# Block 2: context half of the norm on two engines, first transposition of a pair ahead of the scores, query evicted earlier, steps of the first and last column placed anew

## The chip, the cores and the metric

The kernel runs on one core of one Trainium2 chip. The time is device time of one execution, in microseconds (us); a lower one is better. Names of the engines: TensorE (PE, with PEld for its weight loads), VectorE (DVE), ScalarE (ACT), GpSimd (POOL), and SyncE (SP), which issues the weight transfers.

## What is computed

One sequence of 256 tokens of width 1024 goes through two blocks, all in float32. Block 1 (two layers of mixing and feed-forward) is not touched. Block 2 has four layers of kinds A, B, C, A, here called layers 0 to 3, on 256 latent tokens and 256 context tokens:

```
for i in range(4):                      # kinds A, B, C, A
    sh, sc, gt    = split(silu(c) @ ada_w[i] + ada_b[i], 3)
    shc, scc, gtc = split(silu(c_ctx) @ ada_w[i] + ada_b[i], 3)
    h  = rms_norm(x,  norm_g[i]) * (1 + sc)  + sh       # latent half
    hc = rms_norm(xc, norm_g[i]) * (1 + scc) + shc      # context half
    u, z   = split(h @ w_in)            # q, k, v and a gate z
    uc, zc = split(hc @ w_in)
    o, oc  = mixer(u, uc)               # q, k normed per head (A, C: rope), softmax(q k^T) v
    x  = x  + gt  * ((o  * silu(z))  @ w_out)
    xc = xc + gtc * ((oc * silu(zc)) @ w_out)           # not in the last layer
```

Kind A has 16 query heads on 4 key heads, kind B adds a neighbourhood bias, kind C subtracts a second softmax. The last layer needs no context output, so its queries are the 256 latent tokens alone.

## The kernel before

Everything is kept with features on the 128 partitions, in KC = 8 chunks of 128; T = 256 latent and C = 256 context tokens make N2 = 512 columns. Each matrix product is made of three passes (`product`, lines 456 to 460): high part of the weight by high and low part of the activation, and low part of the weight by the high part. So each weight tile has to be split: ACT rounds it to `w_hi` (L1018, `hi_parts`), POOL or DVE subtracts to `w_lo` (L298, `lo_parts`). Tiles come in one fixed order (`PLAN`) through a ring of four; three splits are kept. `chunk` yields after each of the eight k steps of a product, so that the steps can be dealt out between other PE work.

Each engine has its own program of which the order is written out by hand; semaphores connect them. An engine that waits holds all that stands behind it in its program.

**The norm** (`block2`, beginning). DVE multiplies x2 by the reciprocal norm, chunk by chunk (L1706, semaphore `normed`). ACT scales and shifts the latent half of each (L1233, `h_full`), POOL the context half (L2057, `h_ctx`). PE makes the v product from it (L740): its first quarter waits for `h_full` chunk by chunk, its third quarter for all of `h_ctx`. ACT then evicts a row of the next modulation (L1023) and rounds all to `h_hi` (L1240), DVE makes `h_lo` (L1709).

**The columns.** Attention goes over eight columns c (a pair of heads) and in each over NU units u: three token tiles by two heads, NU = 6, in layers 0 to 2; NU = 4 in layer 3. A pair is the two units 2p and 2p + 1. PE per unit (lines 857 to 908): at even u `scores` of both units of the pair (L781, L786), a part of the steps of the matrix products of the next query (`chunk`, "q chunk") and of the gate z (`gemm_part`), transposition of the probabilities of unit u - 2 (`to_keys`, L696) into the one bank `tb`, another part, and at odd u `values_both` of the pair before (L839, L845). `scores` waits until the exponentials of the two units before are done, `to_keys` until that unit's probabilities are normalised (`p_normed`) and the bank `tb` has been read (`t_read`). At u = NU - 2 PE makes the sums of squares of the next query (`q_sums`, L754), which wait for ACT's `q_sq`.

DVE per unit: the maxima of both scores (`biggest`, L1766 and L1763), at even u the copy of the pair's first transposition (`first_keys`, L1811), at odd u the two scalings (`normalise`, L1803); at u = NU - 2 and NU - 1 rope of the next query and its norm sum (`q_rms`, L1742), after which POOL raises it to the power (L2071). The first `biggest` of a column waits for that. ACT per unit: at even u the two exponentials (L1342, L1336), at odd u `second_keys` (L1305), the copy of the pair's second transposition, for which `values_both` waits; then, at u = NU // 2, `evac_q` of the next column: w_hi of a later tile, a square (L1245) and a scaled copy `raw` (L1248) of the query's bank. In kind C a pair gives one combined matrix (`combine`), `keys` (L1298) copies its transposition, and `subln` normalises the column before.

The last column also splits the gated outputs: ACT's `gated_high` (L1289), DVE's `split_gated` (L1844). FILL_SLOT is true in layers 0 to 2; there column 0 and 7 also carry a row of modulation, and `gemm_part` has steps of its own for them.

Of the kernel before, what the change touches and what calls it, by code (L numbers as in the profile page):

```python
# [19 lines left out]
KC = D // P  # L20
T = 256
C = 256
N2 = T + C
# [123 lines left out]
def build_program(nc, wall, consts, pos, x_in, ctx_in, nbias, y_out):  # L147
# [7 lines left out]
    with ExitStack() as stack:  # L155
# [277 lines left out]
        def _(pe):  # L433
# [271 lines left out]
            def block2(L):  # L705
# [151 lines left out]
                for c in range(KC):  # L857
# [22 lines left out]

                    def gemm_part():
                        nonlocal spot
                        if 0 < c < KC - 1 or not slot:
                            steps = (spot + 1) * count // parts - spot * count // parts
                        elif spot < parts // 2:
                            steps = KC // (parts // 2) + (spot < KC % (parts // 2))
                        else:
                            steps = (spot + 1) * 8 // parts - spot * 8 // parts
                        for _ in range(steps):
                            next(pieces, None)  # L890
                        spot += 1
                    for u in range(NU):
                        if u % 2 == 0:
                            scores(c, u)
                        gemm_part()
                        past = [(c, u)] + past[:3]
                        if past[2] and closes(kind, us[past[2][1]]):
                            to_keys(*past[2])
                        if kind != "C":
                            gemm_part()  # L900
                            if past[2] and u % 2:
                                values_both(past[2][0], past[2][1] // 2)
                        elif past[3] and closes(kind, us[past[3][1]]):
                            values(*past[3])
                        if kind == "C" and u == OT and c:
                            out_to_features(c - 1)
                        if u == NU - 2 and c + 1 < KC:
                            q_sums(c + 1)
# [59 lines left out]
        def _(act):  # L968
# [244 lines left out]
            def block2(L):  # L1213
# [17 lines left out]
                for m in range(KC):  # L1231
                    act.wait_ge(S["normed"], (5 + L) * KC + m + 1)
                    act.activation(h2[:, m, 0:T], h2[:, m, 0:T], ACT.Identity, bias=ada[:, L, m, 0:1], scale=mod[:, m, 0:1])\  # L1233
                        .then_inc(S["h_full"], 1)
                for _ in range(FILL_RMS[L]):
                    ada_row_out()
                act.wait_ge(S["h_full"], (6 + L) * KC)
                for m in range(KC):
                    act.wait_ge(S["h_ctx"], L * KC + m + 1)
                    act.activation(h_hi[:, m, :], h2[:, m, :], ACT.Copy).then_inc(S["h_hi_ready"], 1)  # L1240

                def evac_qk(R, dst_sq, gain, signal, N, at=None):
# [114 lines left out]
                for c in range(KC):  # L1357
                    for u in range(NU):
                        if u == 0 and c >= (2 if slot else 1):
                            evac_z(c - slot)  # L1360
                        if u % 2 == 0:
                            exponential(c, u)
                            exponential(c, u + 1)
# [4 lines left out]
                        else:  # L1368
# [3 lines left out]
                                output_squares(past[3][0])  # L1372
                            if u == OT - 1 and c:
                                subln(c - 1)
                        if u == NU // 2 and c + 1 < KC:
                            evac_q(c + 1, early if c == 1 else None)
                            if c == 1 and slot:
                                ada_columns_out()
                        if u == NU // 2 and c == KC - 1 and slot:
                            evac_z(c)  # L1380
                        if c == KC - 1:
# [59 lines left out]
        def _(dve):  # L1441
# [244 lines left out]
            def block2(L):  # L1686
# [180 lines left out]
                past = [None] * 4  # L1867
                for c in range(KC):
                    for u in range(NU):
                        if u % 2 == 0:  # L1870
                            biggest(c, u)
                            biggest(c, u + 1)
                        if u == NU - 1 and c + 1 < KC:
                            q_end(c + 1)
                        past = [(c, u)] + past[:3]
                        if kind == "C" and u % 2:
                            combine(c, u)
                        if kind != "C":
                            if past[2] and u % 2 == 0:
                                first_keys(*past[2])  # L1880
                            if u % 2:
                                normalise(c, u - 1)
                                normalise(c, u)
                        elif past[3] and closes(kind, us[past[3][1]]):
                            output(*past[3])
# [3 lines left out]
                            q_start(c + 1)  # L1889
                        if u == NU - 1 and c + 1 < KC:  # L1890
                            q_rms(c + 1)
                        if c == KC - 1:
                            for i in splits_at(NU, u, FILL_SLOT[L], OT):
                                split_gated(i)
                last = [(KC - 1, u) for u in range(NU) if closes(kind, us[u])]
                if kind == "C":
                    output(*last[-2])
# [59 lines left out]
        def _(pool):  # L1957
# [81 lines left out]
            def block2(L):  # L2039
# [11 lines left out]
                if kind == "B":  # L2051
                    pool.wait_ge(S["h_full"], 6 * KC)
                    for head in range(4):
                        load_bias(head)
                for m in range(KC):
                    pool.wait_ge(S["normed"], (5 + L) * KC + m + 1)
                    pool.tensor_scalar(h2[:, m, T:N2], h2[:, m, T:N2], mod[:, m, 1:2], ada[:, L, m, 1:2], ALU.mult, ALU.add).then_inc(S["h_ctx"], 1)  # L2057
                def qz_tile(i):
# [276 lines left out]
```

## Time and profile before

| | |
|---|---|
| median of three runs | 2235.68 us (2224.66 to 2236.77) |
| the profiled execution | 2232.29 us, span 2230.5 us |
| PE, PEld | 91%, 77% of the span busy |
| DVE, ACT, POOL | 53%, 49%, 42% |
| granted PE clock, mean | 0.951 of full speed |
| block 2 | from about 938 us to the end |

The profile is of one execution. A line of the timeline has start, duration, engine, line of the program, operation, output and inputs with their forms, a count where several were merged, and in brackets the engine's idle time before it with what ended it. "ACTq L1251" is ACT's sequencer at a semaphore instruction on that line. The granted clock is a share of the full rate: 1.00 is 2.4 GHz, 0.50 is 1.2 GHz.

### The profile page before, as it was taken

Reading aid. Unit: us, or ns where it says so; the run is one execution under the profiler, and the core shown is the slowest. Engines: PE = TensorE matmul, PEld = TensorE weight load, DVE = VectorE, ACT = ScalarE, POOL = GpSimd, SP = SyncE. Lnnn points to the kernel's source line nnn. Section 1 sums busy time; section 2 is a strip of 40 time slices with the busy share of each in tenths; the row PEclk is TensorE's granted clock in tenths of the full one; section 3 lists DMA queues with packets and bytes.
Section 4 is the critical chain, followed back from the end, with each engine's and each line's share of the span. In section 5 each row is a group of like instructions: output and inputs, shape, how many; then the busy total and the mean of one; then the engine's idle time right before and its main releaser. Section 6 shows DMA issues by size and latency. Waiting matters only on the chain.

```text
span 2230.5 us, 39126 instructions
## 1 busy us (share of the span) xinstructions
PE 2036.7 (91%) x14528; PEld 1717.4 (77%) x14528; DVE 1187.7 (53%) x2582; ACT 1084.9 (49%) x2073; POOL 933.0 (42%) x598
## 2 busy tenths in 40 slices
PE   6899899988998999888999999998999899798787
PEld 5898799987987899776766886665788667567666
DVE  6854556658545566347673206667223766614553
ACT  5353566453634654454554336445334555535443
POOL 1574378004744682043452123443204455424443
PEclk9899999998999999999999999999999999899898
DMA  7353656653435566442123332222223211223211
GB/s 262 114 152 112 190 172 196 184 186 113 149 101 187 171 188 188 164 142 76 48 61 101 114 104 84 88 67 85 95 86 95 95 38 48 76 95 104 67 58 57
DMA packets 72991, 262.89 MB, mean 118 GB/s; under 512 B 8048, under 2 KB 10224, under 8 KB 72560
## 3 DMA queue, kind: packets, MB, share of 16 engines
q1 hardware_dynamic: 71536, 256.31, 36.6%
q0 software_dynamic: 1280, 4.20, 0.6%
q8 instruction: 116, 1.90, 0.4%
q14 instruction: 59, 0.48, 0.1%
HBM read 259.43 MB, written 1.05 MB: 117 GB/s over the span
## 4 chain that ended last, share of the span: by engine, by line
PE 68%; DVE 9%; issue 8%; POOL 7%; ACT 6%; DMA 1%; DVEq 0%; SPq 0%; ACTq 0%; POOLq 0%
PE gemm L458 15%; PE gemm L459 14%; PE gemm L460 14%; PE gemm L740 7%; POOL w_lo L298 3%; PE tbank L696 2%; PE score L781 2%; PE obank L839 2%; PE stat L703 1%; POOL rot L1970 1%; PE gemm L666 1%; PE stat L536 1%; ACT w_hi L1018 1%; PE stat L754 1%; PE score L786 1%
## 5 line engine op out<-in xcount | busy, mean ns | idle before, releaser
L298 POOL TENSOR_TENSOR w_lo<-ring,w_hi 128x1024 fp32r<-128x1024 f32 x262 | 628.6, 2401 | 721.8 <-ACT w_hi L1018 718.4
L458 PE MATMUL gemm<-g_hi,w_hi 128*128 128x256 f32 x1344 | 394.7, 294 | 29.2 <-DVE w_lo L298 10.8
L1018 ACT ACTIVATE w_hi<-ring 128x1024 fp32r<-128x1024 f32 x344 | 361.3, 1053 | 82.9 <-PE gemm L460 37.4
L458 PE MATMUL gemm<-h_hi,w_hi 128*128 128x512 f32 (+1 forms) x928 | 390.8, 421 | 4.7 <-POOL w_lo L298 4.7
L459 PE MATMUL gemm<-g_lo,w_hi 128*128 128x256 f32 x1344 | 384.0, 286 | 0.0
L460 PE MATMUL gemm<-g_hi,w_lo 128*128 128x256 f32 x1344 | 383.6, 285 | 0.0
L459 PE MATMUL gemm<-h_lo,w_hi 128*128 128x512 f32 (+1 forms) x928 | 352.6, 380 | 0.0
L460 PE MATMUL gemm<-h_hi,w_lo 128*128 128x512 f32 (+1 forms) x928 | 352.1, 379 | 0.0
L458 PEld LDWEIGHTS gemm<-g_hi,w_hi 128*128 128x128 f32 x1344 | 262.9, 196 | 47.7 <-issue 23.3
L460 PEld LDWEIGHTS gemm<-g_hi,w_lo 128*128 128x128 f32 x1344 | 264.2, 197 | 0.0
L459 PEld LDWEIGHTS gemm<-g_lo,w_hi 128*128 128x128 f32 x1344 | 263.3, 196 | 0.1
L458 PEld LDWEIGHTS gemm<-h_hi,w_hi 128*128 128x128 f32 x928 | 181.2, 195 | 92.1 <-issue 62.8
L460 PEld LDWEIGHTS gemm<-h_hi,w_lo 128*128 128x128 f32 x928 | 181.2, 195 | 34.3
L459 PEld LDWEIGHTS gemm<-h_lo,w_hi 128*128 128x128 f32 x928 | 182.0, 196 | 32.2 <-issue 8.4
L1342 ACT ACTIVATE pr<-score,small 128x512 f32<-128x512 f32 (+1 forms) x192 | 127.5, 669 | 160.3 <-DVE small L1768 158.4
L740 PE MATMUL gemm<-ring,arena 128*128 128x128 f32 x1280 | 158.1, 288 | 11.6 <-ACT arena L1233 9.9
L740 PEld LDWEIGHTS gemm<-ring,arena 128*128 128x128 f32 x1280 | 154.4, 201 | 15.2 <-DMA ring<-wall 12.5
L1766 DVE TENSOR_REDUCE small<-score 128x1 f32<-128x512 f32 (+1 forms) x144 | 98.6, 685 | 94.5 <-PE score L781 38.2
L298 DVE TENSOR_TENSOR w_lo<-ring,w_hi 128x1024 fp32r<-128x1024 f32 x82 | 104.0, 1274 | 52.7 <-ACT w_hi L1018 51.6
L696 PE MATMUL tbank<-cst,pr 128*128 128x128 f32 x560 | 89.7, 283 | 25.9 <-DVE pt L1811 25.8
L696 PEld LDWEIGHTS tbank<-cst,pr 128*128 128x128 f32 x560 | 67.7, 144 | 48.6 <-issue 39.1
L1905 DVE TENSOR_TENSOR x<-x,rot 128x512 f32<-128x512 f32 (+1 forms) x32 | 29.7, 927 | 140.4 <-ACTq L1419 140.4
(305 smaller groups left out, 3608.9 us busy)
## 6 DMA issues: line engine op xcount, KB each, us to landing
ring<-wall SPq DMA_DIRECT2D x478, 512.0 KB, 3.7
r<-nbias POOLq DMA_DIRECT2D x16, 256.0 KB, 2.9
cst<-consts SPq DMA_DIRECT2D x1, 2037.0 KB, 13.4
r<-x_t SPq DMA_DIRECT2D x1, 1024.0 KB, 5.8
x<-ctx_t SPq DMA_DIRECT2D x1, 1024.0 KB, 15.8
y_t<-x SPq DMA_DIRECT2D x4, 256.0 KB, 2.4
cst<-consts SPq DMA_DIRECT2D x1, 303.5 KB, 3.0
x<-pos SPq DMA_DIRECT2D x1, 128.0 KB, 2.0
```

The source lines that it names most:

```text
L298: eng.tensor_tensor(w_lo[:, q % SPLITS, :, :], ring[:, t % RING, :, :], w_hi[:, q % SPLITS, :, :].bitcast(F), ALU.subtract)\
L458: pe.matmul(out, w[0][:, k, :], x[0], start=start, stop=False)
L459: pe.matmul(out, w[0][:, k, :], x[1], start=False, stop=False)
L460: return pe.matmul(out, w[1][:, k, :], x[0], start=False, stop=stop)
L696: ins = pe.transpose(tb[:, j * P:(j + 1) * P], src(j), ident)
L740: ins = pe.matmul(out[:, t * P:(t + 1) * P], h2[:, k, t * P:(t + 1) * P], w[:, k, :], start=(k == 0), stop=(k == KC - 1))
L781: ins = pe.matmul(bk[:, :], q[:, t * P:(t + 1) * P], k, start=True, stop=True)
L839: ins = pe.matmul(rows(hh)[:, t * P:(t + 1) * P], v(hh, j), pt[:, hh, j * P:(j + 1) * P], start=(j == 0), stop=(j == 3))
L1018: act.activation(w_hi[:, q % SPLITS, :, :], ring[:, t % RING, :, :], ACT.Copy).then_inc(S["hi_ready"], 1)
L1342: ins = act.activation(dst[:, a:z], src[:, a:z], ACT.Exp, scale=rq, bias=NBm[:, 2 * i4 + q:2 * i4 + q + 1], accum_out=SUM[:, 2 * i4 + q:2 ...
L1766: seq(dve.tensor_reduce(MX[:, i2:i2 + w], bk[:, :] if t < 2 else bk[:, :].rearrange("p (a n) -> p a n", a=2), AX, ALU.max))
L1905: dve.tensor_tensor(x2[:, m, 0:NQ], x2[:, m, 0:NQ], rot[:, m % 2, 0:NQ], ALU.add).then_inc(S["x2_ready"], 1)
```

## The change

Four edits, all in block 2.

1. Norm: POOL does the context half of the even chunks alone; ACT does it for the odd chunks, each right behind the latent half of the same chunk. ACT waits once for all of `h_ctx` ahead of `h_hi`.
2. Kinds A and B: at even u PE transposes unit u - 2 ahead of the scores, where it stood behind them and a part of the products; DVE's `first_keys` stands ahead of `biggest` in the same way. Kind C keeps its order.
3. ACT's `evac_q` of the next column (with the ada columns in column 1) stands at the head of unit NU // 2: ahead of `second_keys` (`keys` and `subln` in kind C), and in layer 3 ahead of two exponentials.
4. First column of layers 0 to 2: the eight steps of the q chunk are made in the first third of the column, where they filled the first half. Last column: DVE makes the splits of the gated outputs of two units together at the odd one.

```diff
@@ PE, gemm_part
-                        if 0 < c < KC - 1 or not slot:
+                        if c == 0 and slot and spot < parts // 2:
+                            steps = KC * 3 // parts * (spot < parts // 3)
+                        elif 0 < c < KC - 1 or not slot:
@@ PE, units
                     for u in range(NU):
+                        past = [(c, u)] + past[:3]
                         if u % 2 == 0:
+                            if kind != "C" and past[2]:
+                                to_keys(*past[2])
                             scores(c, u)
                         gemm_part()
-                        past = [(c, u)] + past[:3]
-                        if past[2] and closes(kind, us[past[2][1]]):
+                        if past[2] and u % 2:
                             to_keys(*past[2])
@@ ACT, norm
+                    if m % 2:
+                        act.activation(h2[:, m, T:N2], h2[:, m, T:N2], ACT.Identity, bias=ada[:, L, m, 1:2], scale=mod[:, m, 1:2])\
+                            .then_inc(S["h_ctx"], 1)
                 for _ in range(FILL_RMS[L]):
                     ada_row_out()
                 act.wait_ge(S["h_full"], (6 + L) * KC)
+                act.wait_ge(S["h_ctx"], (L + 1) * KC)
                 for m in range(KC):
-                    act.wait_ge(S["h_ctx"], L * KC + m + 1)
@@ ACT, units
                         if u == 0 and c >= (2 if slot else 1):
                             evac_z(c - slot)
+                        if u == NU // 2 and c + 1 < KC:
+                            evac_q(c + 1, early if c == 1 else None)
+                            if c == 1 and slot:
+                                ada_columns_out()
                         if u % 2 == 0:
                             exponential(c, u)
                             exponential(c, u + 1)
...
-                        if u == NU // 2 and c + 1 < KC:
-                            evac_q(c + 1, early if c == 1 else None)
-                            if c == 1 and slot:
-                                ada_columns_out()
@@ DVE, units
+                        past = [(c, u)] + past[:3]
                         if u % 2 == 0:
+                            if kind != "C" and past[2]:
+                                first_keys(*past[2])
                             biggest(c, u)
                             biggest(c, u + 1)
...
-                        past = [(c, u)] + past[:3]
...
-                            if past[2] and u % 2 == 0:
-                                first_keys(*past[2])
...
-                        if c == KC - 1:
-                            for i in splits_at(NU, u, FILL_SLOT[L], OT):
-                                split_gated(i)
+                        if c == KC - 1 and u % 2:
+                            for v in (u - 1, u):
+                                for i in splits_at(NU, v, FILL_SLOT[L], OT):
+                                    split_gated(i)
@@ POOL, norm
-                for m in range(KC):
+                for m in range(0, KC, 2):
                     pool.wait_ge(S["normed"], (5 + L) * KC + m + 1)
```

## Rows read from the trace of the kernel before

**Rows 1.** Waits of PE: who waited for whom, us in total, times, longest.

```profile
PE stat L754 <- ACTq L1251: 26.8, 13, 2.9
PE tbank L696 <- DVE pt L1811: 25.8, 23, 4.1
```

**Rows 2.** Busy time by stretch: columns in layers 0, 1, 2, and six of 3.

```profile
core 0: us, PE busy (x) PEld busy (x) DVE busy (x) ACT busy (x) POOL busy (x), PEclk, DMA share, GB/s
1046.00:1067.70 21.70, 21.70 (x137) 15.44 (x137) 15.16 (x38) 11.55 (x26) 10.37 (x6) 1.00 0.17 49
1464.89:1488.04 23.15, 22.05 (x138) 15.38 (x137) 14.71 (x38) 11.38 (x26) 10.06 (x8) 1.00 0.25 69
1855.82:1879.88 24.06, 22.33 (x114) 16.85 (x113) 16.16 (x42) 14.08 (x38) 12.99 (x11) 0.93 0.15 45
2078.66:2179.02 100.36, 84.39 (x651) 68.93 (x649) 57.72 (x143) 46.44 (x95) 45.21 (x35) 0.91 0.20 60
```

**Rows 3.** Timeline (start, us, instruction): norm of layer 1, four engines.

```profile
1247.02 4.87 DVE L1706 TENSOR_TENSOR arena<-x,stat 128x512 f32<-128x512 f32 x8
1247.74 4.79 ACT L1233 ACTIVATE arena<-arena,ada,mod 128x256 f32<-128x256 f32 x8 [2.29 <-DVE arena L1706]
1247.81 4.73 POOL L2057 TENSOR_SCALAR arena<-arena,mod,ada 128x256 f32<-128x256 f32 x8 [18.63 <-DVE arena L1706]
1248.48 11.52 PE L740 MATMUL gemm<-ring,arena 128*128 128x128 f32 x64 [3.31 <-ACT arena L1233]
```

**Rows 4.** Timeline: ACT and PE at unit 3 of a column of layer 0.

```profile
1079.31 0.78 ACT L1342 ACTIVATE pr<-score,small 128x512 f32<-128x512 f32 x1
1081.35 0.60 ACT L1305 ACTIVATE pt<-tbank 128x512 f32<-128x512 f32 x1 [1.18 <-PE tbank L696]
1081.84 1.05 ACT L1018 ACTIVATE w_hi<-ring 128x1024 fp32r<-128x1024 f32 x1
1082.79 0.59 ACT L1245 ACTIVATE sq<-gemm 128x512 f32<-128x512 f32 x1
1083.41 0.69 ACT L1248 ACTIVATE raw<-gemm,cst 128x512 f32<-128x512 f32 x1
...
1082.00 1.09 PE L839 MATMUL obank<-pt,arena 128*64 128x128 f32 x16
```

**Rows 5.** Timeline: the same place in layer 1.

```profile
1453.59 0.72 ACT L1336 ACTIVATE pr<-scratch,small 128x512 f32<-128x512 f32 x1 [0.80 <-DVE small L1763]
1454.30 0.63 PE L696 MATMUL tbank<-cst,pr 128*128 128x128 f32 x4 [0.66 <-DVE pt L1811]
1455.61 1.10 PE L839 MATMUL obank<-pt,arena 128*64 128x128 f32 x16
```

**Rows 6.** Busy time and granted clock: a wait in layer 1; after waits, layers 3, 2.

```profile
1384.00:1388.00 4.00, 1.83 (x26) 1.00 (x26) 3.82 (x7) 2.55 (x6) 3.00 (x3) 1.00 0.42 131
2125.50:2129.50 4.00, 4.00 (x31) 3.45 (x31) 2.28 (x7) 2.09 (x4) 2.20 (x4) 0.60 0.48 135
1863.40:1866.90 3.50, 3.50 (x10) 2.83 (x10) 2.38 (x7) 1.50 (x6) 1.69 (x2) 0.51 0.44 150
```

**Rows 7.** Timeline: norm sum of the next query in a column of layer 2.

```profile
1868.09 0.16 DVE L1742 TENSOR_SCALAR small<-stat 128x8 f32<-128x8 f32 x1
```

**Rows 8.** Timeline: PE and ACT in layer 3, column 0 and a later one.

```profile
2066.53 1.13 PE L781 MATMUL score<-arena,d 64*128 64x512 f32 x4 [3.38 <-ACT pr L1342]
...
2112.61 1.13 PE L781 MATMUL score<-arena,d 64*128 64x512 f32 x4
2118.65 1.13 PE L781 MATMUL score<-arena,d 64*128 64x512 f32 x4
2124.39 0.61 PE L754 MATMUL stat<-cst,sq 128*128 128x2 f32 x4 [2.57 <-ACTq L1251]
...
2123.75 0.47 ACT L1248 ACTIVATE raw<-gemm,cst 128x256 f32<-128x256 f32 x1
```

**Rows 9.** Timeline: a scaling on DVE beside a split on POOL, layer 1.

```profile
1386.38 2.04 DVE L1803 TENSOR_SCALAR pr<-pr,small 128x512 f32<-128x512 f32 x1
1385.75 2.37 POOL L298 TENSOR_TENSOR w_lo<-ring,w_hi 128x1024 fp32r<-128x1024 f32 x1
```

## The prediction

> **What bounds the kernel now.** I read the page's share of each engine first: TensorE (PE) is busy for 91% of the span, so a change off PE's path is worth only the PE time that it frees or takes. Then the waits of PE. Two kinds bear on this diff, 26.8 us in 13 waits for the sums of the query's squares (`q_sums`, L754), each until ScalarE's (ACT's) `evac_q` has signalled, and 25.8 us in 23 waits of a transposition (L696) for VectorE's (DVE's) copy of the one before, `first_keys` [rows 1]. Then busy time by column, where it is seen that the waits are unevenly spread. A middle column of layer 0 takes 21.70 us with PE busy in all of it at full granted clock; one of layer 1 takes 23.15 us with 1.1 us idle; one of layer 2 24.06 us at a clock of 0.93; the six of layer 3 take 100.36, 16.73 each, at 0.91 with 16 us idle in sum [rows 2]. So layer 0 can only lose in its columns, and layer 3 has most to gain.
>
> **Norm's context half.** In layer 1's norm DVE makes eight products in 4.87 us, ACT scales the latent halves in 4.79, GpSimd (POOL) the context halves in 4.73, both at DVE's pace, and both end within 0.1 us of 1252.5. PE begins the v product after a wait of 3.31 us and takes each chunk as ACT frees it [rows 3]. POOL was not late, so nothing is won there. Now ACT has 12 operations of 4.79 / 8 = 0.60 in place of 8. The last latent chunk is the eleventh of them: 11 x 0.60 = 6.6 us after the start against 4.8, so PE has it 1.8 us later, while the last context chunk (7.2 us) is there before PE comes to the third quarter of the tile. Layers 1 to 3 pay 3 x 1.8 = 5.4. Layer 0 doesn't: there PE starts v late, for its weights. The later `h_hi` (2.4 us) is covered by the v tiles of two or eight times 7 us. Bounds: 0 to +10, the upper one if each of the three longer waits also holds PE at the half clock for one more stretch (below). I take +5.4.
>
> **Query evicted sooner, layers 0 and 1.** Here NU is 6, so u == NU // 2 is 3, an odd unit, and at odd units no exponential follows: the move puts `evac_q` ahead of `second_keys`, not of an exponential. What is queued behind it is ACT's copy of the second transposition of the pair, and PE's `values_both` waits for that. In layer 0 ACT's second exponential ends at 1080.1, the copy runs at 1081.35 to 1081.9 after 1.18 us idle, and PE begins the values at 1082.00, in time by 0.1. Then follow w_hi (1.05), the square (0.59) and raw (0.69), 2.3 us in all [rows 4]. In the new order these 2.3 us start when the exponentials end. Those end 0.36 later relative to PE's order, since the first transposition (four matmuls, 0.36 start to start) now stands ahead of the scores. So: 1080.1 + 0.4 + 2.3 = 1082.8, copy until 1083.4 and 0.15 of signals, 1083.55: PE waits 1.55 us, in a column that had no idle time. Columns 2 to 6: 5 x 1.55 = 7.8. In column 1 the query's tile has a reserved place and no w_hi, but the ada columns follow (0.4 us): +0.6. Column 0 is a chain of scores, exponential, scores; moving its matrix steps forward fills no wait that isn't opened again later, and 1.3 us of ACT work stand ahead of the copy: +0.8. The last column has no `evac_q`: the pair's first copy now comes first on DVE, its second scores' maxima 0.65 later, and the values wait for ACT behind them: +0.6. The first transposition's own wait, p_normed of unit u - 2, is met 0.7 us or more before PE arrives, and the deferred splits of the gated products fill DVE idle time: 0. Layer 0: +9.8; bounds +4 (half of each wait absorbed) to +14.
>
> In layer 1 the maxima take longer (the bias is added), so the second exponential ends at 1454.4, as late as PE's second transposition, which waited 0.66 us for `first_keys`; the values begin at 1455.61 [rows 5]. That wait of 0.66 and its like of 0.45 at unit 1 go. But 1454.4 + 0.4 + 2.3 + 0.75 gives values at 1457.8, 2.1 later than before and some 2.8 of it in one idle stretch. Of the 0.45 only half is won, as ACT's copy ends last there. Net +1.9 in five columns, 9.5; column 1 +0.9, column 0 +0.8, the last +0.4: +11.6.
>
> **The clock.** A wait of 2.03 us (1384.4 to 1386.4) left the granted clock at 1.00, that is at 2.4 GHz. After the wait for the q sums in layer 3 the stretch from 2125.5 to 2129.5 has 0.60, after layer 2's wait of 1.60 and the tiny matmuls behind it the next 3.5 us have 0.51, so the lower level, 1.2 GHz, nearly throughout [rows 6]. A fall costs about half of such a stretch, 1.7 us. I price layer 0's new waits (1.55) at no fall and layer 1's (2.8) at a fall in four of five: +6.8, bounds 0 and +10. Layer 1: +18.4.
>
> **Layer 2 (kind C).** The order of transpositions and scores stays; only `evac_q` moves, ahead of `keys` and of `subln`. PE's wait of 1.60 for the q sums goes and with it the fall, 3.3 us per column. Next late is the reciprocal norm of the query: DVE's L1742 stands at 1868.09 behind the combination of the column's last pair, which itself waits for exponentials and for rope [rows 7]; POOL's power takes 1.65 more before the next column's first maximum. That chain moves forward only by 1.0 us, and the scores of the next pair wait behind it. I take 1.8 of the 3.3, five columns, and 0.4 for a sixth: -9.4; bounds -4 to -17.
>
> **Layer 3 (kind A, NU 4).** Here unit 2 is even, so `evac_q` goes ahead of two exponentials, into time in which ACT is idle: its raw copy at 2123.75 was what the q sums (2.57 us) waited for, while the q chunk was complete before the scores at 2118.65 [rows 8]. New: the chunk's end, w_hi, square and raw (about 2 us) end before the exponentials can start. The wait goes, and so does the fall. The half column without wait takes 6.04 us (2112.61 to 2118.65); the other would be that and 0.45 for the sums: 12.5. The next thing late is rq for the next column (DVE, then POOL 1.0) by 0.1 to 0.3. I take 12.8 against 16.73, six columns: -23.6. Column 0, from 2057.51 to 2078.66, holds a wait of 3.38 [rows 8], 2.54 for the sums and seven us at the lower clock: -5.5. The last +0.5. Layer 3: -28.6; bounds -8 (next rival) and -32.
>
> **Where the port comes in.** DVE's scaling of 512 columns takes 0.49 as a rule; it took 2.04 at 1386.38, and it ended with POOL's w_lo of 1385.75 to 1388.1 [rows 9]. With `evac_q` earlier, w_hi and so w_lo shift by up to 5 us and could fall on layer 3's scalings. I place w_lo at 2.0 to 4.4 us and 6.1 to 8.5 of a column of 12.8, the scalings at 3.6 and 10.8: one is held for 0.9 us, 1.2 us ahead of its reader. Forecast: no cost. The Trainium skill ("GPSIMD Engine Reference", section "Key points") says that POOL shares its SBUF interfaces with DVE and contends with DVE instructions in a 2-port perf mode or with two SBUF inputs; rows 9 agree, and by that rule a scaling is exposed wherever w_lo lands, which is the last rival. By the same rule norm's products, with one input in PSUM, were never disturbed by POOL, as their even 0.61 us shows; so relieving POOL there would bring nothing.
>
> **Sum** against the profiled execution (2232.29; span 2230.5 and 1.8 around it): +5.4 + 9.8 + 18.4 - 9.4 - 28.6 = -4.4, 2227.9. The median of the runs shown, 2235.68, lies 3.4 above that execution; I add most of it and predict **2231**.
>
> **Rivals.**
> 1. *The loss in layers 0 and 1 is smaller*: no fall in layer 1 (-6.8) and half of each new wait absorbed in layer 0 (-5): 2219. For it: 2.03 us left the clock alone [rows 6]. Against: ACT's queue is strictly in order [rows 4].
> 2. *Every new wait brings a fall*: layer 0 +9, layer 1 +2, norm +4: 2246. Against: 1.55 is under the 2.03 that did no harm; for it: 1.60 in layer 2 did, with thin work beside it.
> 3. *Slower: w_lo lands on the scalings of layer 3*. Both of a pair held, 2 x (2.04 - 0.49) = 3.1 us per column [rows 9], and first transpositions now wait for them ahead of the scores: six columns, +19, 2250. It decides from the point at which a scaling ends over 1.2 us later than I place it.
> 4. *The reorder wins nothing in layer 3* because an exponential bounds the column: excluded nearly, ACT is busy for 46 of 100 us there [rows 2].
>
> **Chances.** Forecast 0.42 (2223 to 2240), rival 1 0.30 (2207 to 2224), rival 2 0.12, rival 3 0.16. A measurement of this kernel tells about 0.5% from no change, here 11 us. Faster by more: nearly all of rival 1 and a little of the forecast, 0.32; slower by more: most of rival 3 and a third of rival 2, 0.19; within: 0.49. Range 2211 to 2250.
>
> **What would show it.** Right: `values_both` (L839) waiting for ACT L1305 at unit 3 in each column of layers 0 and 1, about 1.5 and 2.8 us; L696's waits for L1811 gone except in the last columns; L754's waits gone in layers 2 and 3; layer 3's columns near 12.8; the v product's last latent chunk 1.8 us later. Wrong: layer 0's columns still 21.7, or layer 3's above 15 with L1803 over 1 us.

## The result: slower by half a per cent

The changed kernel takes 2240.5 us (median of 12, 2235.2 to 2246.8) where the kernel before takes 2231.9 (12, 2221.8 to 2241.7). The ratio is 1.0047, with a 95% interval of 1.0033 to 1.0062: about 10 us slower. I had forecast -4.4 us, 2231. The time lies in my range, the sign was wrong.

Its profiled execution has a span of 2236.7 us, +6.2. The page, first its span and PE's share, then the groups of the values and of the transposition (busy, mean ns of one, idle before):

```profile
span 2236.7 us, 39126 instructions
...
PE 2032.4 (91%) x14528; PEld 1711.3 (77%) x14528; DVE 1180.7 (53%) x2582; ACT 1087.6 (49%) x2089; POOL 927.0 (41%) x582
...
L839 PE MATMUL obank<-pt,arena 128*64 128x128 f32 x768 | 59.3, 303 | 52.6 <-ACT pt L1312 52.6
L696 PE MATMUL tbank<-cst,pr 128*128 128x128 f32 x560 | 95.0, 293 | 10.7 <-DVE pr L1810 6.3
```

In this kernel's numbering ACT's copy is L1312 (it was L1305), w_hi L1022, the square L1252, the raw copy L1255, DVE's scaling L1810 and its copy L1818. The 26.8 us of waits for the q sums are gone, and of the 25.8 us for `first_keys` [rows 1] 4.4 are left; with 6.3 for DVE's scaling, which stands ahead of that copy, the transposition waits 10.7. In their place `values_both` (L839), which waited 2.3 us in all before, waits 52.6 us, and always for ACT's copy: as much as the other two together had been.

Busy time of the middle columns after (columns 2 to 6 of layers 0, 1 and 2, columns 1 to 6 of layer 3; each line has the stretch, its length, busy time by engine with instructions, granted clock, DMA share, GB/s):

```profile
1050.00:1168.90 118.90, 110.69 (x684) 78.09 (x682) 78.88 (x185) 58.21 (x126) 52.14 (x31) 1.00 0.15 45
1434.90:1571.30 136.40, 118.53 (x681) 83.50 (x680) 75.39 (x190) 56.69 (x125) 49.53 (x34) 0.94 0.18 55
1835.80:1949.40 113.60, 104.61 (x562) 78.00 (x562) 77.92 (x206) 69.34 (x186) 64.96 (x55) 1.00 0.16 47
2110.20:2187.00 76.80, 76.60 (x652) 61.06 (x650) 53.19 (x144) 46.76 (x96) 47.11 (x35) 1.00 0.27 83
```

Divided by the number of columns and set against [rows 2]: layer 0 23.8 us where it was 21.7; layer 1 27.3 (23.15), at a clock of 0.94; layer 2 22.7 (24.06), at 1.00; layer 3 12.8 (16.73), with hardly any idle time and at 1.00. The stages of the profiled executions, from the start of column 0's first scores to that of column 7's, beside my forecast:

| stage | before | after | change | forecast |
|---|---|---|---|---|
| up to layer 0's column 0 | 1001.1 | 998.4 | -2.7 | 0 |
| layer 0 | 155.3 | 170.5 | +15.2 | +9.2 |
| layer 1 | 160.1 | 186.2 | +26.1 | +18.0 |
| layer 2 | 165.3 | 157.9 | -7.4 | -9.4 |
| layer 3 | 121.5 | 95.5 | -26.0 | -29.1 |
| last columns, norms and the rest | 627.1 | 628.2 | +1.1 | +6.9 |

The last row holds norm (+5.4) and the three last columns (+0.6, +0.4, +0.5) of my sum; over all kernels of this study it lies between 626 and 631 us. The first row is no effect of the change: over all kernels of this study that stretch ends between 994 and 1010 us, so one execution's span tells nothing finer than some 10 us. I therefore read parts from the stages and the whole from the intervals. Middle columns of the same code repeat to 0.1 us in layer 0, nearly so in layers 1 and 2, where single columns stand out by 0.3 to 1.2. Those of layer 3 in the kernel before do not: they take 15.5 to 18.7 us, nearly all with a wait of some 2.57 and at clocks of 0.83 to 0.99, so 16.73 is the mean of unlike columns. The first column of a layer isn't steady either (28.5 us here in layer 0, 26.3 and 26.2 in two other kernels).

### The profile page after: what moved, and what is told of

Read it like the earlier page. It is cut to its first block, busy times and chain, and to the rows that moved or that the text cites. A ratio compares the mean times of both kernels' runs of the same rounds, so it can differ in the third digit from the quotient of the medians.

```text
span 2236.7 us, 39126 instructions
## 1 busy us (share of the span) xinstructions
PE 2032.4 (91%) x14528; PEld 1711.3 (77%) x14528; DVE 1180.7 (53%) x2582; ACT 1087.6 (49%) x2089; POOL 927.0 (41%) x582
## 4 chain that ended last, share of the span: by engine, by line
PE 69%; DVE 10%; ACT 9%; issue 6%; POOL 4%; DMA 1%; ACTq 0%; DVEq 0%; SPq 0%; POOLq 0%
PE gemm L458 15%; PE gemm L460 14%; PE gemm L459 14%; PE gemm L740 7%; PE tbank L696 3%; PE score L781 2%; PE obank L839 2%; POOL w_lo L298 1%; PE stat L703 1%; ACT w_hi L1022 1%; ACT pr L1349 1%; POOL rot L1978 1%; DVE small L1773 1%; PE score L786 1%; PE gemm L666 1%
## 5 line engine op out<-in xcount | busy, mean ns | idle before, releaser
L1022 ACT ACTIVATE w_hi<-ring 128x1024 fp32r<-128x1024 f32 x344 | 361.3, 1053 | 82.3 <-PE gemm L460 38.1
L458 PE MATMUL gemm<-h_hi,w_hi 128*128 128x512 f32 (+1 forms) x928 | 380.0, 410 | 4.7 <-POOL w_lo L298 4.7
L459 PE MATMUL gemm<-h_lo,w_hi 128*128 128x512 f32 (+1 forms) x928 | 347.6, 375 | 0.0
L460 PE MATMUL gemm<-h_hi,w_lo 128*128 128x512 f32 (+1 forms) x928 | 347.5, 374 | 0.0
L839 PE MATMUL obank<-pt,arena 128*64 128x128 f32 x768 | 59.3, 303 | 52.6 <-ACT pt L1312 52.6
L696 PE MATMUL tbank<-cst,pr 128*128 128x128 f32 x560 | 95.0, 293 | 10.7 <-DVE pr L1810 6.3
L1978 POOL TENSOR_TENSOR rot<-shf,cst 128x512 f32<-128x512 f32 (+1 forms) x36 | 46.2, 1284 | 139.0 <-DVE shf L1493 138.8
```

What stands on the lines that cost most here:

```text
L458: pe.matmul(out, w[0][:, k, :], x[0], start=start, stop=False)
L459: pe.matmul(out, w[0][:, k, :], x[1], start=False, stop=False)
L460: return pe.matmul(out, w[1][:, k, :], x[0], start=False, stop=stop)
L696: ins = pe.transpose(tb[:, j * P:(j + 1) * P], src(j), ident)
L839: ins = pe.matmul(rows(hh)[:, t * P:(t + 1) * P], v(hh, j), pt[:, hh, j * P:(j + 1) * P], start=(j == 0), stop=(j == 3))
L1022: act.activation(w_hi[:, q % SPLITS, :, :], ring[:, t % RING, :, :], ACT.Copy).then_inc(S["hi_ready"], 1)
```

## Where the new wait comes from

ACT and PE at unit 3 of a column of layer 0, after:

```profile
1082.80 0.78 ACT L1349 ACTIVATE pr<-score,small 128x512 f32<-128x512 f32 x1 [3.79 <-DVE small L1775]
...
1084.42 1.05 ACT L1022 ACTIVATE w_hi<-ring 128x1024 fp32r<-128x1024 f32 x1
1085.37 0.59 ACT L1252 ACTIVATE sq<-gemm 128x512 f32<-128x512 f32 x1
1085.99 0.69 ACT L1255 ACTIVATE raw<-gemm,cst 128x512 f32<-128x512 f32 x1
1086.92 0.60 ACT L1312 ACTIVATE pt<-tbank 128x512 f32<-128x512 f32 x1 [0.25 <-ACT raw L1255]
...
1084.63 0.60 PE L696 MATMUL tbank<-cst,pr 128*128 128x128 f32 x4
...
1087.57 1.09 PE L839 MATMUL obank<-pt,arena 128*64 128x128 f32 x16 [1.64 <-ACT pt L1312]
```

PE finished the transposition at 1085.2, ACT could have copied it then, and copied it at 1086.92, behind w_hi, square and raw copy. That is [rows 4] in another order, and the wait is 1.64 us in each of five columns (forecast: 1.55). The same place in layer 1, against [rows 5]:

```profile
1474.63 1.04 ACT L1022 ACTIVATE w_hi<-ring 128x1024 fp32r<-128x1024 f32 x1
...
1477.12 0.60 ACT L1312 ACTIVATE pt<-tbank 128x512 f32<-128x512 f32 x1 [0.25 <-ACT raw L1255]
...
1477.77 1.47 PE L839 MATMUL obank<-pt,arena 128*64 128x128 f32 x16 [3.12 <-ACT pt L1312]
1479.17 1.12 PE L696 MATMUL tbank<-cst,pr 128*128 128x128 f32 x4
```

Here the wait is 3.12 us, and what follows runs at half rate: the transposition takes 1.12 us for its usual 0.66.

## Experiments

Theory Q: the loss comes from ACT's queue, `evac_q` ahead of `second_keys`. Rival O: it comes from the new order of transposition and scores on PE and DVE. All times below are set against runs of the kernel before on the same chip.

**The early query only where an exponential follows.**

```diff
-                        if u == NU // 2 and c + 1 < KC:
+                        if u == NU // 2 and ((NU // 2) % 2 == 0 or kind == "C") and c + 1 < KC:
                             evac_q(c + 1, early if c == 1 else None)
...
+                        if u == NU // 2 and not ((NU // 2) % 2 == 0 or kind == "C") and c + 1 < KC:
+                            evac_q(c + 1, early if c == 1 else None)
```

> The changed kernel, but the query is evicted sooner only where the unit NU // 2 is even or the layer is of kind C (layers 2 and 3); in layers 0 and 1 the eviction stands behind second_keys again. Theory Q (ACT's queue order: the 2.3 us of w_hi, square and raw copy ahead of the pair's second copy): the waits of values_both at unit 3 (1.64 us in layer 0, 3.12 in layer 1) go, and with them layer 1's clock falls. A middle column of layer 0 takes 22.1 us (the 0.44 that PE's new order costs stays), one of layer 1 22.5, layers 2 and 3 stay at 22.7 and 12.9. The whole falls by 35 to 42 us against the changed kernel, to about 2200. Rival O (the new order on PE and DVE makes the waits): the columns stay at 23.8 and 27.2 and the time at 2240.

Measured: 2208.7 us, ratio 0.989 (0.9863 to 0.9916) to the kernel before, some 35 us under the changed kernel. Middle columns of layers 0 and 1:

```profile
1050.20:1160.80 110.60, 110.60 (x683) 78.07 (x682) 78.85 (x185) 58.20 (x126) 51.98 (x31) 1.00 0.16 49
...
1425.00:1541.00 116.00, 110.68 (x683) 78.04 (x682) 75.39 (x190) 56.23 (x126) 49.14 (x34) 1.00 0.21 64
```

22.1 us and 23.2 us for a column. Theory Q holds for the large part of the loss, and rival O's 23.8 and 27.2 are out. But layer 1 was to reach 22.5 and did not; the next run has the same 23.1 to 23.2 and shows what PE waits for there.

**The order of transposition and scores alone.**

```diff
+                        past = [(c, u)] + past[:3]
                         if u % 2 == 0:
+                            if kind != "C" and past[2]:
+                                to_keys(*past[2])
                             scores(c, u)
                         gemm_part()
-                        past = [(c, u)] + past[:3]
-                        if past[2] and closes(kind, us[past[2][1]]):
+                        if past[2] and u % 2:
                             to_keys(*past[2])
...
```

On DVE `first_keys` moves ahead of `biggest` in the same way.

> The kernel before with one part alone: the pair's first transposition (and DVE's copy of it) ahead of the scores. Theory Q: PE pays 0.24 us for each transposition that is followed by scores instead of a matrix step, less a saved switch, 0.44 us per column: 22.1 in layer 0; in layer 1 the waits of 0.45 and 0.66 for first_keys go, so 23.15 - 1.11 + 0.44 = 22.5; layer 3 keeps its waits for the q sums, 16.5 to 17. In sum -1 to -3 us: 2230. Rival O: layer 0's columns take 23.8 and layer 1's over 26, 2250 or more.

Measured: 2247.8 us, ratio 1.0068 (1.0040 to 1.0096): 15 us slower, where I expected 1 to 3 faster. The columns are 22.1 in layer 0, as expected, but 23.2 in layer 1 and 17.9 in layer 3. Busy time of layer 3's columns 1 to 6, and PE's waits in layer 3 (us in total, times, longest):

```profile
2093.40:2200.50 107.10, 88.62 (x650) 71.81 (x649) 59.83 (x144) 46.84 (x96) 47.53 (x37) 0.89 0.20 60
...
PE stat L754 <- ACTq L1253: 20.2, 7, 3.3
```

Without the early query the new order only makes the waits for the q sums longer: 20.2 us in seven, most of them 3.03, where they were 2.57 [rows 8]. In layer 1 the waits for `first_keys` of 0.45 and 0.66 went, and PE waits for ACT's copies instead, 0.39 at L845 and 0.61 at L839: 1.11 us became 1.00. By stage, layer 0 lost 2.5 us, layer 1 1.4 and layer 3 6.6; layer 2, whose order the edit doesn't touch, took 2.0 more in this execution. And the order has a price of its own, which I had not put in my sum. PE's weight loads in layer 0: first in the changed kernel, where scores follow the transposition; then in the kernel before, where a product follows it:

```profile
1080.08 0.42 PEld L696 LDWEIGHTS tbank<-cst,pr 128*128 128x128 f32 x4 [0.39 <-DVE pr L1810]
1080.67 0.30 PEld L781 LDWEIGHTS score<-arena,d 64*128 64x128 f32 x4 [0.17 <-issue]
```

```profile
1077.95 0.59 PEld L696 LDWEIGHTS tbank<-cst,pr 128*128 128x128 f32 x4
1078.51 0.19 PEld L458 LDWEIGHTS gemm<-h_hi,w_hi 128*128 128x128 f32 x1
```

Before, the transposition's weights were being loaded at 1077.95, 0.23 us ahead of its first matmul at 1078.18, beside the product's last matmul, and the next work began 0.35 us after it (1078.53). Now the loads of the scores start together with the scores' own first matmul, at 1080.67, 0.59 us after the transposition began. That is 0.24 us three times in a column, less what is saved where products are no longer interrupted; the column shows 0.4 in sum (22.1 against 21.7). Most of the 0.24 lies ahead of the scores: 0.20 us from the last of the four transposition matmuls to their first, where a product's follows after 0.03. The rest goes with the transposition's own load, which behind values starts with its matmul too (1080.08) and not ahead of it. The Trainium skill ("TensorE: Matmul & The Clock Gate", section "Step-by-step: what each phase is for") says that PE pulls weight loads ahead of running matmuls where their row groups don't conflict or where they go to the background weight buffer. The trace has loads 0.23 us ahead behind products, and none ahead for the scores or for a transposition behind values; why not there, no run here shows.

**The early query alone.** The edit is the second half of the change on ACT, in all layers, with everything else as before.

> The kernel before with one part alone: the query evicted sooner in all layers. Theory Q: values_both waits at unit 3 in layer 0 for 1.3 to 1.6 us (columns of 23.2), in layer 1 for 2.5 to 3.1 us and with a clock fall (columns of 26.5); layer 2's columns take 22.7; layer 3's 13.0 to 13.5. In sum about +8 + 20 - 7 - 22 = -1: 2231. Rival O: layers 0 and 1 keep 21.7 and 23.2, and the time is 2205.

Measured: 2225.9 us, ratio 0.9961 (0.9942 to 0.9979). This part alone is a gain of 9 us: layer 3 94.3 us from column 0 to 7 (121.5 before), layer 2 158.4 (165.3), against layer 0's 162.6 (155.3) and layer 1's 176.0 (160.1). The waits at L839 are 1.20 in layer 0 and 1.83 in layer 1, both shorter than in the changed kernel (1.64 and 3.12). Layer 1's middle columns took 26.5, 25.0, 26.6, 25.0 and 25.0 us, with the same waits in each. The stretches around the wait in two neighbours (the wait and what is just ahead of it, then the 4 us behind it):

```profile
1468.10:1471.30 3.20, 1.33 (x8) 0.88 (x8) 2.89 (x5) 2.86 (x6) 2.02 (x1) 1.00 0.29 82
1471.30:1475.30 4.00, 4.00 (x35) 3.14 (x35) 2.44 (x6) 0.71 (x3) 0.42 (x1) 1.00 0.48 135
...
1493.10:1496.30 3.20, 1.34 (x9) 0.90 (x9) 2.89 (x5) 2.85 (x6) 2.03 (x1) 1.00 0.23 82
1496.30:1500.30 4.00, 4.00 (x27) 2.83 (x28) 1.71 (x5) 0.00 (x0) 0.41 (x1) 0.65 0.47 135
```

Equal work and an equal wait, and the clock fell behind one and not behind the other. Whether a wait of this size costs a fall (1.6 us here, 26.6 against 25.0) can't be told from its length.

**How long a wait may be.** The changed kernel, with the query's square repeated on ACT ahead of the copy, one to four times (`more`) in columns 3 to 6 of layer 0.

```diff
                     seq(act.activation(dst_sq, b[:, 0:N], ACT.Square))
+                    for _ in range(more):
+                        seq(act.activation(dst_sq, b[:, 0:N], ACT.Square))
```

> The changed kernel, with ACT's square of the query repeated 1, 2, 3 and 4 times more ahead of second_keys in columns 3, 4, 5 and 6 of layer 0 (the same values again), each 0.59 us. Theory Q: the wait of values_both grows from 1.64 by 0.59 each to 2.2, 2.8, 3.4 and 4.0, the column of 23.8 as much. Theory W (the wait's length decides on the clock, near 2 us): from the second on a half-clock stretch follows each, 1.7 us more. Rival P (the length alone doesn't decide: in query_only the same wait of 1.83 us was followed by the lower clock in every second column only): falls in some of these columns whatever the order of lengths.

One execution, 2252.5 us. The waits were 1.64, 2.28, 2.90, 3.53 and 4.16 us. The five columns:

```profile
1055.20:1079.00 23.80, 22.16 (x139) 15.65 (x138) 15.77 (x37) 11.56 (x25) 10.46 (x7) 1.00 0.15 45
1079.00:1103.40 24.40, 22.12 (x139) 15.60 (x138) 15.77 (x37) 12.17 (x26) 10.40 (x7) 1.00 0.14 44
1103.40:1128.40 25.00, 22.10 (x139) 15.58 (x138) 15.78 (x37) 12.76 (x27) 10.41 (x7) 1.00 0.15 43
1128.40:1155.60 27.20, 23.67 (x137) 16.78 (x136) 15.77 (x37) 13.36 (x28) 10.38 (x7) 0.94 0.13 39
1155.60:1183.30 27.70, 23.54 (x139) 16.67 (x138) 15.78 (x37) 14.38 (x30) 10.49 (x7) 0.94 0.12 39
```

Up to 2.90 us a column grows by 0.6 us, as much as its wait, and the clock stays at 1.00. At 3.53 it grows by 2.2: the wait's 0.6 and 1.6 for the fall; at 4.16 by another 0.4. So theory Q's arithmetic is right to 0.1 us. Theory W is wrong on the length (near 2 us). In layer 0 the clock fell behind the longer waits alone, 3.53 and 4.16, but in layer 1 it fell behind some waits of 1.83 and layer 2, before the change, behind each of 1.60 [rows 6]. So the length alone doesn't decide; what else does, these runs don't settle.

**Norm's half alone.** The edit moves four of the eight context scalings of a norm from POOL to ACT, as in the change.

> The kernel before with one part alone: half of the context scalings on ACT. If the pace of one ACT scaling alone (0.54 and 0.49 us) sets the chunks, a pair takes 1.48 us and the last latent chunk comes 0.84 us later: +0.7 us in each of layers 1 to 3, +2 in all. If my first reckoning by 0.60 was right, 1.8 each, +5.4. If PE's later wait costs a clock fall too, 2.5 each.

One execution, 2239.9 us (before: median 2233.6). ACT in layer 1's norm (latent halves L1233, context halves L1236):

```profile
1251.54 1.20 ACT L1233 ACTIVATE arena<-arena,ada,mod 128x256 f32<-128x256 f32 x2 [2.29 <-DVE arena L1709]
1252.64 0.58 ACT L1236 ACTIVATE arena<-arena,ada,mod 128x256 f32<-128x256 f32 x1
1253.13 1.08 ACT L1233 ACTIVATE arena<-arena,ada,mod 128x256 f32<-128x256 f32 x2
1254.11 0.58 ACT L1236 ACTIVATE arena<-arena,ada,mod 128x256 f32<-128x256 f32 x1
```

Three operations take 1.47 us (1252.64 to 1254.11), 0.49 each. The last latent half ends at 1257.15, 5.6 us after the first began, where it was 4.8 [rows 3]: 0.8 later, not 1.8. PE's stretch from the last matmul of the norm's sums (L703) to the first of the ada columns (L516) takes 17.6 us on the mean of layers 1 to 3 where it took 16.9 in the kernel before; over the five kernels with this edit the mean is 17.6 to 18.1, over the seven without it 16.8 to 17.3. So some 0.7 us in a layer, up to 1.2.

**The repacing of column 0 alone.**

```diff
+                        if c == 0 and slot and spot < parts // 2:
+                            steps = KC * 3 // parts * (spot < parts // 3)
-                        if 0 < c < KC - 1 or not slot:
+                        elif 0 < c < KC - 1 or not slot:
```

> The kernel before with one part alone: column 0's matrix steps moved forward in layers 0 to 2 (nine in the first third of the places). By my first reckoning nothing is won and nothing lost: column 0 of layer 0 23.2 us, of layer 1 20.8, to +-0.5. If the repacing was what made columns 0 slower (28.5 and 24.6 in the changed kernel, 24.1 and 23.1 in query_only), they take 24.5 and 22 or more.

(The places hold eight steps, not nine.) One execution, 2243.1 us (before: median 2230.7, highest 2239.7). Column 0 of layer 0 took 22.9 us (23.2), that of layer 2 21.5 (21.2), that of layer 1 23.3 in place of 20.8. The column, and PE's wait in it:

```profile
1379.92:1403.20 23.28, 19.24 (x163) 12.96 (x162) 17.33 (x40) 11.79 (x26) 6.36 (x6) 0.85 0.31 100
...
1392.13 1.09 PE L696 MATMUL tbank<-cst,pr 128*128 128x128 f32 x4 [3.48 <-DVE pt L1813]
```

Before, PE waited 1.50 us for the exponential and 2.03 for the copy, with matrix steps between them, at a clock of 1.00. With those steps done earlier both waits are one of 3.48 us. The sum is the same to 0.05 us, and the clock is 0.85. My +-0 was right for the waits and wrong for the column. The kernel with norm and repacing (below) repeats it, 23.2 us at 0.85, and the four kernels with none of the column edits in this layer have 20.8 at 1.00. But this is not what the repacing does in the change, where the early query and the new order are there too: see the columns 0 below.

**Two and two.** The four parts in pairs, to see whether they add up.

> The kernel before with two parts: the query evicted sooner in all layers and the first transposition ahead of the scores; norm and pacing as before. Theory I (the two parts harm each other in layers 0 and 1: PE no longer waits for first_keys, so it reaches the values earlier and the longer wait brings the lower clock every time): layer 0's columns 23.8 us and layer 1's 27.2, as in the changed kernel, more than the sum of the parts alone (layer 0: 21.7 + 0.4 + 1.2 = 23.3, layer 1: 23.2 + 0 + 2.5 = 25.7). The rest of the changed kernel's loss is then norm's and the repacing's, so the time is 4 to 7 us under the changed kernel's: about 2235. Rival A (the parts add): 23.3 and 25.7, about 2225.

> The kernel before with the two other parts: norm's context half on two engines and column 0 repaced. Theory I: norm 0.5 to 1 us in each of three layers, layer 1's column 0 23.2 in place of 20.8 by the clock: +4 to +6 us, ratio 1.002 to 1.003. Rival A (that column's 23.2 was a chance of one execution): column 0 at 20.8 and +2 in all, ratio 1.001.

| | layer 0, middle column | layer 1, middle column | ratio to before |
|---|---|---|---|
| query alone | 22.9 | 25.0 or 26.6 | 0.9961 (0.9942 to 0.9979) |
| order alone | 22.1 | 23.1 | 1.0068 (1.0040 to 1.0096) |
| query and order | 23.8 | 27.2 | 1.0004 (0.9977 to 1.0030) |
| norm and repacing | 21.7 | 23.2 | 1.0040 (1.0019 to 1.0061) |
| all four (the change) | 23.8 | 27.2 | 1.0047 (1.0033 to 1.0062) |

The medians were 2235.3 us for query and order, as expected, and 2243.5 for norm and repacing, where I expected +4 to +6. The expected sums of the columns were 23.3 and 25.7. Query and order do harm each other in layers 0 and 1, as theory I said: the columns take 23.8 and 27.2. In layer 0 the cause can be read off. From a pair's scores to its `values_both` the chain over DVE and ACT takes 6.90 us with the old order and with the new (1058.43 to 1065.33 in the early query alone, 1080.67 to 1087.57 in the change). A transposition stood within it and now stands ahead of it; that is 0.44 us less for PE to do meanwhile, and PE waits 1.64 for 1.20. In layer 1 there was also a stop of 0.67 us for `first_keys` within it, which is gone: 3.12 for 1.83, the former with a fall in every column. In layer 3 they help each other: the order costs 6.6 us without the early query (128.1 against 121.5) and gains with it (12.8 for 13.3 in a middle column). The two pairs together make 1.0044, the change 1.0047. Norm and repacing cost 9 us by the timed runs (4 to 14), more than the 2 to 4 of norm and the 2.4 of layer 1's column 0 that I can point to; the rest is open.

The columns 0 (us, granted clock), in one execution of each:

| | layer 0 | layer 1 |
|---|---|---|
| before | 23.2, 0.93 | 20.8, 1.00 |
| query alone | 24.1, 0.93 | 23.1, 0.93 |
| order alone | 24.6, 0.93 | 21.8, 1.00 |
| query and order | 26.2, 0.93 | 24.6, 0.93 |
| norm and repacing | 23.0, 0.93 | 23.2, 0.85 |
| all four (the change) | 28.5, 0.82 | 24.6, 0.93 |

In layer 1 query and order give the 24.6 of the change by themselves, so the repacing adds nothing there.

**The part that pays, alone.** The kernel before, with the early query in layers 2 and 3 and nothing else; then the same with the new order in columns 1 to 6 of layer 3.

```diff
+                        if u == NU // 2 and ((NU // 2) % 2 == 0 or kind == "C") and c + 1 < KC:
+                            evac_q(c + 1, early if c == 1 else None)
```

```diff
+                        ahead = NU == 4 and 0 < c < KC - 1
+                            if ahead and past[2]:
+                                to_keys(*past[2])
```

> The kernel before with one edit: the query is evicted sooner in layers 2 and 3 alone (kind C, and NU // 2 even); norm, transpositions and pacing as before. Theory S (the parts add up by stage): layers 0 and 1 as before (155 and 160 us from the first to the last column), layer 2 158.4 against 165.3, layer 3 94.3 against 121.5 as in query_only; -34 us from the columns, +1.7 at the end: about 2200, ratio 0.985. Rival: layer 3's gain needs the new order of transpositions, as its columns of 12.8 against 13.3 and the first copy's wait of 0.60 might say: then over 105 us and 2210.

> The same and, in the middle columns of layer 3 alone (1 to 6), the first transposition ahead of the scores. Theory S: column 0 keeps its 15.5 us (18.8 with the new order) and the last its shorter waits, the middle ones take 12.8 in place of 13.3: another -2 to -3 us, 2197; from the time alone that can't be told from the run beside it, from the windows it can. Rival: 15.5 was an accident of the clock and not of the order; then column 0 takes 18.8 here too.

Measured: 2198.8 us, ratio 0.9854 (0.9828 to 0.9880), and 2200.2 us, ratio 0.9856 (0.9834 to 0.9879). The middle columns of layers 1 and 2, and those of layer 3, in the first of them:

```profile
1413.10:1528.90 115.80, 110.26 (x683) 76.88 (x681) 73.54 (x190) 56.93 (x125) 49.25 (x34) 1.00 0.22 65
1788.90:1902.50 113.60, 104.62 (x562) 78.01 (x562) 77.94 (x206) 69.37 (x186) 64.94 (x55) 1.00 0.16 47
...
2062.40:2141.20 78.80, 75.93 (x651) 61.68 (x648) 52.62 (x141) 46.84 (x97) 46.56 (x35) 1.00 0.26 81
```

Layer 1 as before, layers 2 and 3 with their gain: 32 us faster than the kernel before and, by the medians, 42 than the change. The stages add up as theory S said. The order in layer 3's middle columns gives 12.7 for 13.3 and 93.8 us for 95.9 in the layer, and nothing that the time shows. Of column 0 the rival was half right: it took 17.1 and 17.7 us in these two kernels with the old order and 15.5 with the early query alone, all with the same two waits (2.8 us ahead of it and 3.3 or 3.4 in it), at clocks of 0.80, 0.81 and 0.89. Query and order, with the new order there, had 16.0 at 0.89. So the 15.5 was the clock, not the order.

## Why the prediction was wrong

**Layer 3: right.** -26.0 for columns 0 to 7 against -29.1, with middle columns of 12.8 as forecast. The half column of 6.04 without a wait was the right measure. All that fell short is column 0: -2.3 in place of -5.5, 18.8 us in place of 15.6, for its long waits stay and the clock is 0.73 there. The edits in the columns don't fix that clock: query and order alone had 16.0 at 0.89.

**Layer 2: right** within its bounds, -7.4 against -9.4: the five middle columns gain 1.6 each, not 1.8, and column 0 lost 0.5.

**Layer 1: the term was too small**, +26.1 against +18.0. The wait came as forecast (3.12 against 2.8), and a fall with each (I took four of five). What failed is the credit: I let the waits of 0.45 and 0.66 go and won 0.66 and half of 0.45 back. The run of the order alone shows that PE then waits 1.00 us for ACT, so the order won nothing here, and the column lost 4.1 us in place of 3.3: 2.5 without the fall, where I had 1.9, and 1.6 for a fall each time. The rest came in the two columns ahead of them: +1.6 in column 1, where I had 0.9, and +3.7 in column 0, where I had 0.8 and no fall. The clock there is 0.93 for 1.00. The early query alone brings that column to 23.1 at 0.93, and with the new order to the 24.6 of the change; I had sought the fall in the middle columns only.

**Layer 0: a term was missing**, +15.2 against +9.2. The wait was sized to 0.1 us (1.64 against 1.55). Not in the sum was what PE's own order costs, 0.4 us in each column: I counted four matmuls at 0.36 from start to start, a figure taken from where a product follows them, and scores follow now. Column 0 took 28.5 us in place of 24.0. Its waits of over 0.5 us grew from one of 3.63 us to 7.1 in sum (2.25, 3.66, 0.53 and 0.69), and its clock went from 0.93 to 0.82; two other kernels with the same two parts had 26.2 and 26.3 there, so some 2 us of it are this execution's. My 0.8 was right for the early query alone (+0.9). The order alone costs 1.4 there, and both together 3.0.

**Norm: the size was off**, the mechanism right. The 0.60 us that I multiplied by 11 was DVE's pace, which ACT kept to, and not what one ACT operation takes (0.49 from start to start). The last latent half came 0.8 us later, not 1.8. Yet norm and repacing cost 9 us in the timed runs, so the two small terms together were no smaller than I said.

**The rivals.** Rival 1, a smaller loss in layers 0 and 1, to which I gave 0.30, was the opposite of what happened, and with it went my 0.32 for faster. Rival 2 was near: falls came in layer 1 and in the first columns, though none in layer 0's middle ones. Rival 3 (w_lo on the scalings) didn't come: no scaling (L1810) of layer 3 was held, all took about 0.5 us. The Trainium skill's rule that POOL shares its SBUF interfaces with DVE ("GPSIMD Engine Reference", section "Key points") could not be seen there, for w_lo and a scaling met for 0.18 us at most, and the scaling took its 0.49. In layer 0 scalings were held beside POOL's other work, at 1.3 to 1.6 us for 0.49, off PE's path before and after.

**The step that failed.** The new waits were sized well, 1.64 for 1.55 and 3.12 for 2.8, and they were sized for PE's new position. What failed in the first place is the columns 0, for which my sum has +0.8, +0.8 and -5.5 for layers 0, 1 and 3, measured +5.3, +3.7 and -2.3. That is 10.6 us, as much as the whole error (-4.4 forecast, +6.2 between the profiled executions), though some 2 us of it in layer 0 and up to 2.8 in layer 3 differ between kernels with the same edits in the columns. Next come layer 1's middle columns (20.7 for 16.3), where the credit for the order was not paid out, and the order's own price in layer 0, which I put at nothing (2.0 us). That the time still lay in my range is in part luck: the stage of the last columns and norms came out 5.8 us under my forecast and hid as much of the loss.

## What to carry over

A queue that runs in order has one good place for a long job: ahead of work whose input isn't there yet, never ahead of a copy that is already due. The same line of a shared loop can be the one in one layer and the other in the next (here by the parity of NU // 2), so ask it for each layer. When an edit takes a wait away from an engine, look for what was ready only because of that wait. Reckon the first column of a loop by its own waits, not as a middle one with a small extra. And price a short operation from the trace between the neighbours that it will have, not those that it has.

## What the hardware showed unexpectedly

- A wait of 1.83 us, with the same work before and behind it, was followed by the lower clock (1.2 GHz) in some columns and not in others; in layer 0 waits up to 2.90 us were not, 3.53 and 4.16 were. A fall cost 1.6 us.
- Two waits of 1.50 and 2.03 us with matrix steps between them left the clock at 1.00; joined to one of 3.48 us they left the column at 0.85 and 2.4 us longer, in two kernels. With a third wait of 1.03 us behind them (the early query alone) the clock was 0.93 though they stayed apart.
- Four 128-row transpositions take 0.35 us from start to start of what follows if that is a 128-row product, 0.59 if it is scores with 64-row weights, whose load starts only with their first matmul (the transposition stood behind a product in the first case and behind values in the second).
